# One gate transfer per group of eight experts, and activations weighed two at a time in column blocks one to four

## The chip, the cores and the metric

The kernel runs on one core of one Trainium2 chip. The metric is the device time of one execution in microseconds (us); lower is better. The kernel as it stands takes 3545.93 us (median of three runs). A profile of one further execution is used for all readings of the trace.

## The reference

A decoder block on 1024 tokens with 1024 channels: two token mixers (chunked retention and a short gated convolution), then a product-key expert retrieval layer (PEER), a per-layer embedding gate and a final norm. Only the PEER layer matters here. For each token eight heads choose 16 experts each out of 16384 and give them softmax gates; then

```python
def block(args):
    xb, ib, gb = args                    # tokens, chosen experts, their gates
    ue = jnp.take(u, ib, axis=0)
    act = jax.nn.gelu(jnp.einsum('td,ted->te', xb, ue), approximate=False)
    ve = jnp.take(v, ib, axis=0)
    return jnp.einsum('te,ted->td', (gb * act), ve)
```

## The kernel before, in words

The 1024 tokens are split. For 384 of them the rows of u and v that they chose are gathered one by one and multiplied on VectorE ("dots"). For the other 640 the layer is computed densely: the 16384 experts are 128 tiles of 128. A tile here is what the text calls an expert. A first stage multiplies every u tile with the 640 tokens, takes the GELU and writes the result (128 x 640, 320 KB) to `act_d` in DRAM. The gates of those tokens, zero for experts that were not chosen, are in `gate_d` in DRAM, laid out as block of 32 tokens, partition, expert, token.

The second stage is the one around the change. It takes the experts in 16 groups of eight (`NGRP`, `EG`), and for each group makes eight column blocks of the output (`dt` 0 to 7; one column block is called a step). In a step TensorE does 48 matmuls (line L1037: eight experts, high and low halves of a float32, two halves of the tokens) into one of two PSUM buffers `main`, and VectorE adds it into the result (`drain`, L2190). While the steps of group b run, the activations of group b+1 are made ready, expert by expert, through one PSUM buffer (`h_ps`, shown as `scr` in the trace):

1. SyncE loads the activation from `act_d` (`load_act`, L608), and ScalarE copies it to PSUM (`h_stage`, L1438).
2. VectorE multiplies it with the gates in `gate_in` (`weigh`, L2179).
3. ScalarE rounds it to the high half (`h_cast`, L1442).
4. VectorE subtracts for the low half (`lo_of_group`, L2184). Only then may `h_stage` of the next expert begin.

Which experts are treated in which step is a table:

```python
WEIGH_AT = ((), (0,), (1,), (2, 3), (4,), (5,), (6, 7), ())
```

The engines work through lists written out by hand, in order. VectorE, per step: drain, then for each expert in the table weigh, one dot (L1807), low half; then the remaining dots of the step (264 dots over 123 steps). ScalarE, per step: `h_stage` of the first expert in the table, then in even steps `v_cast` (L1429) of the two v tiles that TensorE needs two steps later, then `h_cast` of that expert, then the second expert if there is one. GpSimd waits for those casts, makes the low halves of the two v tiles (`v_lo`, L733) and then issues the gathers of rows for the next dots (L686). SyncE loads the next v tile (L568, 512 KB) when a low half is made, and between those loads the activations. Three times (before steps 8 and 72 and at 125) TensorE also turns back a block of the gathered tokens (L1015), which VectorE adds (L2197).

The gates of a group come on ScalarE's queue in two transfers of 1280 KB, each into its own half of the buffer: `load_gates(b + 1, 0)` behind `h_cast` of expert 3, `load_gates(b + 1, 1)` behind `h_cast` of expert 7 (L1421). Before the second stage, the gates of group 0 are read in five parts (L1483).

Of the kernel before, what the change touches and what calls it, by code (L numbers as in the profile page):

```python
# [23 lines left out]
F32 = mybir.dt.float32  # L24
# [3 lines left out]
ALU = mybir.AluOpType  # L28
# [3 lines left out]
P = 128  # L32
# [12 lines left out]
NE = NKEYS  # L45
# [25 lines left out]
TB = 32  # L71
NBLK = TDN // TB
EG = 8
HG = EG // 2
NGRP = NE // EG
# [20 lines left out]
GATE_PARTS = 5  # L96
# [1 line left out]
LAST_ROWS = 2 * S1 + NE - 3  # L98
SHIFT_ROWS = 2 * S1 + NE - 16
FIRST_H = NE - EG  # L100
WEIGH_AT = ((), (0,), (1,), (2, 3), (4,), (5,), (6, 7), ())
ROW_STEPS = V_STEPS - 5


# [55 lines left out]
def filled(step):  # L160

    return 8 + step + sum(1 for at in TURNS if at < step)
# [110 lines left out]
def build(nc, x_t, p_t, stream, u_rows, v_rows, key_t, gains, conv_c, rope, head_c, shape_c, out_t,  # L273
          score_d, act_d, gate_d, res_d):
    with ExitStack() as ctx:
        def sem(name):
            return ctx.enter_context(nc.semaphore(name))
# [26 lines left out]
        lay = region(const0)  # L304
# [10 lines left out]
        lay = region(ring0)  # L315
# [3 lines left out]
        lay = region(set1)  # L319
        a_hi, a_lo = [None] * 2, [None] * 2  # L320
        mix_hi, mix_lo = [None] * 2, [None] * 2
        for ps in range(2):
            lay = region(set1)
            a_hi[ps] = lay(f"a_hi{ps}", [P, DC, WIDTH[ps]], F32R)
            a_lo[ps] = lay(f"a_lo{ps}", [P, DC, WIDTH[ps]], F32R)
            lay = region(set2)
            mix_hi[ps] = lay(f"mix_hi{ps}", [P, DC, WIDTH[ps]], F32R)
            mix_lo[ps] = lay(f"mix_lo{ps}", [P, DC, WIDTH[ps]], F32R)
        lay = region(res0)
# [3 lines left out]
        for k, w in enumerate((TS, TDN, T)):  # L333
            lay = region(tmp0)
            nt0.append(lay(f"nt0_{k}", [P, w], F32))
            rowb.append(lay(f"rowb{k}", [P, 4, w], F32))
            if k < 2:
                lay = region(tmp0)
# [11 lines left out]
        for ps in range(2):  # L350
            w, n = WIDTH[ps], CHUNKS[ps]
            lay = region(set2)
# [10 lines left out]
            lay = region(set2 + 12 * w * 4)  # L363
            y.append(lay(f"y{ps}", [P, 2, w], F32))
            g.append(lay(f"g{ps}", [P, 2, w], F32))
        lay = region(set2 + 40 * 1024)
# [5 lines left out]
        lay = region(set2 + 48 * 1024)  # L372
        atok = [lay(f"atok{t}", [P, D], F32) for t in range(2)]
        s_ix = lay("s_ix", [P, NS, PH, 3 * TOPK], U32)
        lay = region(set2 + 61 * 1024)
        s_gate = lay("s_gate", [P, NS, P], F32)
        s_dot = lay("s_dot", [P, NS, P], F32)
        lay = region(set2 + 30 * 1024)
        keys0 = lay("keys0", [P, 2 * PH, NKEYS], F32)
        lay = region(tmp0 + 12800)  # L380
# [5 lines left out]
        lay = region(set1 + 40 * 1024)  # L386
        sc = lay("sc", [P, NS, 2 * PH, NKEYS], F32)
        lay = region(set1 + 40 * 1024)
# [5 lines left out]
        lay = region(set1)  # L394
        scores = lay("scores", [P, PH * 2, NKEYS], F32)
        gbuf = [lay(f"gbuf{i}", [P, NKEYS, TB], F32) for i in range(2)]
        lay = region(set1 + 2 * K4)
# [4 lines left out]
        lay = region(tmp0)  # L402
# [15 lines left out]
        for u in range(2):  # L418
            at = set1 if u == 0 else set2
            lay = region(at)  # L420
# [3 lines left out]
            lay = region(at + 40 * 1024)  # L424
# [1 line left out]
            v_lo.append(lay(f"v_lo{u}", [P, 2, D], F32R))  # L426
        v_raw = nc.alloc_sbuf_tensor_at("v_raw", [P, PRE, D], F32, offset=set1 + 48 * 1024)
        lay = region(tmp0)
        gate_in = [lay(f"gate_in{i}", [P, NBLK, HG, TB], F32) for i in range(2)]
        lay = region(set2 + 14 * K4)  # L430
        p_raw = lay("p_raw", [P, 2, T], F32)
        lay = region(set1 + 8 * K4)
        ple = lay("ple", [P, DC, T], F32)
        fg = nc.alloc_sbuf_tensor_at("fg", [P, 2, T], F32, offset=set1)
        lay = region(set1)
# [4 lines left out]
        lay = region(set2)  # L440
# [105 lines left out]
        v_hi_made = sem("v_hi_made")  # L546
        v_split = sem("v_split")
        act_in = [sem(f"act_in{k}") for k in range(EG)]
        gate_ins = [sem("gate_ins0"), sem("gate_ins1")]
        h_staged = sem("h_staged")  # L550
        h32_ready = sem("h32_ready")
        hhi_ready = sem("hhi_ready")
        h_ready = sem("h_ready")
        b_filled = sem("b_filled")
# [10 lines left out]
        @block.sync  # L565
        def _(sp):
            def load(pair, s):
                sp.dma_start(raw[:, s, :], stream[bass.ds(2 * pair + s, 1)].rearrange("a p n -> p (a n)")) \  # L568
                    .then_inc(raw_in[s], 16)

            def load_x(ps):
                for c in range(DC):
                    sp.dma_start(res[:, c, START[ps]:START[ps] + WIDTH[ps]],
                                 x_t[c * P:(c + 1) * P, START[ps]:START[ps] + WIDTH[ps]]).then_inc(x_in[ps][c], 16)

            def load_rope(ps):
                for dst, row in ((cos, 0), (sin, 1)):
                    sp.dma_start(dst[ps][:, :], rope[row, :, START[ps]:START[ps] + WIDTH[ps]]).then_inc(rope_in[ps], 16)

            load_x(0)  # L580
            load(0, 0)
            sp.dma_start(gain[:, :, :], gains).then_inc(consts_in, 16)
            load(0, 1)
            sp.dma_start(ident[:, :], shape_c[0]).then_inc(consts_in, 16)
            sp.dma_start(iota[:, :], shape_c[1]).then_inc(consts_in, 16)
            sp.dma_start(convc[:, :, :], conv_c).then_inc(consts_in, 16)
            load_rope(0)
            load_x(1)
            load_rope(1)
            with sp.Fori(1, S1) as pair:  # L590
                for s in range(2):
                    sp.wait_ge(tile_split, 2 * pair + s - 1)
                    load(pair, s)
            with sp.Fori(0, S1) as i:
                for s in range(2):
                    sp.wait_ge(tile_split, 2 * S1 + 2 * i + s - 1)
                    load(i, s)
            with sp.Fori(S1, B_PAIR - S1) as row:
                for s in range(2):
                    sp.wait_ge(tile_split, 2 * S1 + 2 * row + s - 1)  # L600
                    load(row, s)


            for s in range(2):
                sp.wait_ge(tile_split, 2 * B_PAIR + s - 1)
                load(B_PAIR - S1 + PRE // 2, s)
            def load_act(b, k):
                sp.dma_start(h32[b % 2][:, k, :], act_d[EG * (b - 1) + k]).then_inc(act_in[k], 16)  # L608

            sp.wait_ge(tile_done, 2 * B_PAIR)  # L610
            for q in act_st:
                sp.wait_ge(q, 16 + 16 * (FIRST_H // 2))
            for n in range(PRE + 2, NE + 2):
                b, place = divmod(n - 4, EG)
                if 0 <= place < 6 and n >= 4 and b + 1 < NGRP:
                    if place == 0:
                        if b:
                            sp.wait_ge(b_filled, filled(EG * b))
                        load_act(b + 1, 0)
                        load_act(b + 1, 1)  # L620
                    else:
                        load_act(b + 1, place + 1)
                        if place == 5:
                            load_act(b + 1, place + 2)
                sp.wait_ge(v_split, n - 1)
                load(B_PAIR - S1 + n // 2, n % 2)
            for t in range(2 * DC):
                sp.wait_ge(tile_split, F_TILE + t - 1)
                load(F_PAIR - S1 + t % DC // 2, t % 2)
            for half in range(2):  # L630
                at = slice(half * HALF, (half + 1) * HALF)
                for c in range(DC):
                    sp.wait_ge(out_ready, DC * half + c + 1)
                    sp.dma_start(out_t[c * P:(c + 1) * P, at], res[:, c, at]).then_inc(out_st, 16)
            sp.wait_ge(out_st, 16 * 2 * DC)
# [469 lines left out]
        def _(act):  # L1105
# [310 lines left out]
                act.wait_ge(dot_done, P * (t + 1))  # L1416
                act.activation(s_dot[:, t, :], s_dot[:, t, :], ACT.Gelu).then_inc(s_gelu, 1)

            def load_gates(b, half):
                at = EG * (b - 1) + HG * half  # L1420
                act.dma_start(gate_in[half][:, :, :, :].rearrange("p b e t -> p b (e t)"),  # L1421
                              gate_d[:, :, at:at + HG, :].rearrange("b p e t -> p b (e t)")) \
                    .then_inc(gate_ins[half], 16)

            def v_cast(n):
                if n >= 4:
# [13 lines left out]
            def h_cast(b, k):  # L1440
                act.wait_ge(h32_ready, EG * b + k + 1)
                act.copy(h_hi[b % 2][:, k, :], h_ps[:, 0:TDN]).then_inc(hhi_ready, 1)  # L1442
                if k % HG == HG - 1 and b + 1 < NGRP:
                    load_gates(b + 1, k // HG)

            swap_at = min(m for m in range(16 * ND) if due(2 * S1 + tile_of(m) - 1) > 2 * P)
            for e in range(NE):
# [5 lines left out]
                if e > FIRST_H:  # L1453
                    h_cast(0, e - FIRST_H - 1)
                if e >= FIRST_H:
                    h_stage(0, e - FIRST_H)
                j, k = divmod(e - LEAD, SPAN)
# [21 lines left out]
                first = e - (LEAD + SPAN * (ND - 1) + QUARTERS[15] + 2)  # L1479
                for part in range(2 * first, min(2 * first + 2, GATE_PARTS)) if first >= 0 else ():  # L1480
                    blocks = slice(NBLK * part // GATE_PARTS, NBLK * (part + 1) // GATE_PARTS)
                    for half in range(2):
                        act.dma_start(gate_in[half][:, blocks, :, :].rearrange("p b e t -> p b (e t)"),  # L1483
                                      gate_d[blocks, :, FIRST_H + HG * half:FIRST_H + HG * (half + 1), :].rearrange("b p e t -> p b (e t)")) \
                            .then_inc(gate_ins[half], 16)
                if e == NE - 8:
                    act.wait_ge(dot_done, LAST_LOW + 1)
                    for k in range(PRE):
# [1 line left out]
                if NE - PRE - 3 <= e < NE - 3:  # L1490
                    k = e - (NE - PRE - 3)
# [13 lines left out]
            for b in range(NGRP):  # L1505
                for dt in range(DC):
                    step = DC * b + dt
                    if step - 1 in ENDS:
                        sums_out(ENDS.index(step - 1))
                    ks = WEIGH_AT[dt] if b + 1 < NGRP else ()  # L1510
                    for k in ks[:1]:
# [60 lines left out]
            for t in range(2 * DC):  # L1572
                half, n = divmod(t, DC)
                at, s = slice(half * HALF, (half + 1) * HALF), t % 2
# [15 lines left out]
        def _(dve):  # L1590
# [580 lines left out]
                        hots(16 * (j + 1), w)  # L2171

            def weigh(b, k):
                half = k // HG
                if k % HG == 0:
                    dve.wait_ge(gate_ins[half], 16 * (b + GATE_PARTS))
                dve.wait_ge(h_staged, EG * b + k + 1)
                h3 = h_ps[:, 0:TDN].rearrange("p (b t) -> p b t", t=TB)
                dve.tensor_tensor(h3, h3, gate_in[half][:, :, k % HG, :], ALU.mult).then_inc(h32_ready, 1)  # L2179

            def lo_of_group(b, k):
                u = b % 2
# [26 lines left out]
            for step in range(V_STEPS - DC):  # L2209
                b, dt = divmod(step, DC)  # L2210
# [70 lines left out]
            for t in range(2 * DC):  # L2281
                half, n = divmod(t, DC)
                at, s = slice(half * HALF, (half + 1) * HALF), t % 2
# [108 lines left out]
```

## Time and profile before

| | |
|---|---|
| median of 3 runs | 3545.93 us (3545.28 to 3547.40) |
| profiled execution, its own time | 3540.74 us |
| span in the profile | 3538.9 us |
| TensorE busy | 3391.1 us, 96% |
| VectorE, ScalarE, GpSimd busy | 2532.9, 1287.8, 2175.7 us |
| granted TensorE clock, mean | 0.983 of full speed |
| second stage of the PEER layer (L1037) | from 2467.5 to 3381.9 us |

The profiled execution spent 1.8 us outside its span. In the timeline rows the columns are start, duration, engine, line, operation, written tile from read tile, and in brackets the idle time before it with what ended it. DMA packets are counted per queue: q0 holds the gathered rows, q1 what SyncE issues, q10 what ScalarE issues.

### The profile page before, as it was taken

Reading aid. Unit: us, or ns where it says so; the run is one execution under the profiler, and the core shown is the slowest. Engines: PE = TensorE matmul, PEld = TensorE weight load, DVE = VectorE, ACT = ScalarE, POOL = GpSimd, SP = SyncE. Lnnn points to the kernel's source line nnn. Section 1 sums busy time; section 2 is a strip of 40 time slices with the busy share of each in tenths; the row PEclk is TensorE's granted clock in tenths of the full one; section 3 lists DMA queues with packets and bytes.
Section 4 is the critical chain, followed back from the end, with each engine's and each line's share of the span. In section 5 each row is a group of like instructions: output and inputs, shape, how many; then the busy total and the mean of one; then the engine's idle time right before and its main releaser. Section 6 shows DMA issues by size and latency. Waiting matters only on the chain.

```text
span 3538.9 us, 58475 instructions
## 1 busy us (share of the span) xinstructions
PE 3391.1 (96%) x22379; PEld 3332.5 (94%) x22379; DVE 2532.9 (72%) x4232; ACT 1287.8 (36%) x2013; POOL 2175.7 (61%) x1426
## 2 busy tenths in 40 slices
PE   7899989998999989999999999999999999999987
PEld 6899979988999979999999999999999999999975
DVE  5615467668887667898989899754667676767567
ACT  3310131232121232456565655653333333333242
POOL 5578865332678656566666666765566665666544
PEclk9999989999999999999999999999999999999998
DMA  4233432111589868789898988988999998999712
GB/s 153 81 116 122 136 114 79 57 50 60 184 311 316 279 218 310 252 306 335 306 331 309 328 313 311 319 299 284 337 318 334 341 321 304 320 333 320 271 48 95
DMA packets 324309, 851.18 MB, mean 241 GB/s; under 512 B 27665, under 2 KB 125457, under 8 KB 320785
## 3 DMA queue, kind: packets, MB, share of 16 engines
q0 software_dynamic: 110592, 402.70, 31.2%
q1 hardware_dynamic: 92160, 300.62, 25.6%
q10 hardware_dynamic: 121360, 145.25, 12.2%
q8 instruction: 122, 2.00, 0.2%
q14 instruction: 75, 0.61, 0.0%
HBM read 756.20 MB, written 92.27 MB: 240 GB/s over the span
## 4 chain that ended last, share of the span: by engine, by line
PE 84%; DVE 10%; ACT 2%; issue 2%; DMA 1%; POOL 1%; ACTq 0%; DVEq 0%; SPq 0%; POOLq 0%
PE main L777 53%; PE main L1037 24%; PE scr L975 4%; DMA rows<-v_rows,s_idx 1%; DVE rows L1800 1%; PE scr L875 1%; PE scr L792 1%; DVE rowb L1624 1%; PE main L1079 1%; PE scr L816 0%; DVE res L2286 0%; DVE y L1884 0%; PE scr L820 0%; DVE rowb L2010 0%; DVE rowb L1600 0%
## 5 line engine op out<-in xcount | busy, mean ns | idle before, releaser
L653 POOL TENSOR_TENSOR w_lo<-raw,w_hi 128x1024 fp32r<-128x1024 f32 x206 | 534.3, 2594 | 421.9 <-ACT w_hi L1132 417.9
L777 PE MATMUL main<-mix_hi,w_hi 128*128 128x320 f32 (+1 forms) x2816 | 685.2, 317 | 29.8 <-DVE mix_lo L1632 9.9
L777 PE MATMUL main<-mix_lo,w_hi 128*128 128x320 f32 (+1 forms) x2816 | 673.2, 313 | 0.0
L777 PE MATMUL main<-mix_hi,w_lo 128*128 128x320 f32 (+1 forms) x2816 | 673.1, 313 | 0.0
L1807 DVE SCALAR_TENSOR_TENSOR scr<-rows,s_dot,scr 128x1024 f32<-128x1024 f32 x381 | 489.0, 1284 | 167.0 <-DMA rows<-v_rows,s_idx 150.6
L777 PEld LDWEIGHTS main<-mix_hi,w_hi 128*128 128x128 f32 x2816 | 476.8, 190 | 34.5 <-issue 19.6
L777 PE MATMUL main<-a_hi,w_hi 128*128 128x320 f32 (+1 forms) x1728 | 465.8, 324 | 24.2 <-DVE a_lo L1632 8.6
L686 POOL DMA_INDIRECT rows<-u_rows,s_idx x384 | 397.4, 1035 | 135.8 <-issue 69.0
L777 PEld LDWEIGHTS main<-mix_lo,w_hi 128*128 128x128 f32 x2816 | 480.3, 189 | 0.0
L777 PEld LDWEIGHTS main<-mix_hi,w_lo 128*128 128x128 f32 x2816 | 479.5, 189 | 0.0
L1037 PE MATMUL main<-h_hi,v_hi 128*128 128x320 f32 x2048 | 467.7, 310 | 9.3 <-issue 3.5
L1800 DVE CUSTOM_DVE_ANT_0 rows<-rows,scr 128x1024 f32<-128x1024 f32 x384 | 446.1, 1215 | 41.4 <-PE main L777 22.7
L1037 PE MATMUL main<-h_lo,v_hi 128*128 128x320 f32 x2048 | 467.4, 309 | 0.0
L1037 PE MATMUL main<-h_hi,v_lo 128*128 128x320 f32 x2048 | 467.0, 309 | 0.0
L733 POOL TENSOR_TENSOR v_lo<-raw,v_hi 128x1024 fp32r<-128x1024 f32 x126 | 301.8, 2415 | 264.3 <-ACT v_hi L1429 257.9
L777 PE MATMUL main<-a_lo,w_hi 128*128 128x320 f32 (+1 forms) x1728 | 458.9, 320 | 0.0
L777 PE MATMUL main<-a_hi,w_lo 128*128 128x320 f32 (+1 forms) x1728 | 458.3, 320 | 0.0
L686 POOL DMA_INDIRECT rows<-v_rows,s_idx x384 | 368.9, 961 | 126.8 <-issue 82.9
L1037 PEld LDWEIGHTS main<-h_hi,v_hi 128*128 128x128 f32 x2048 | 342.5, 188 | 10.5 <-issue 4.0
L1037 PEld LDWEIGHTS main<-h_hi,v_lo 128*128 128x128 f32 x2048 | 343.0, 188 | 0.0
L1037 PEld LDWEIGHTS main<-h_lo,v_hi 128*128 128x128 f32 x2048 | 343.0, 188 | 0.0
L777 PEld LDWEIGHTS main<-a_hi,w_hi 128*128 128x128 f32 x1728 | 302.9, 190 | 32.6 <-issue 19.0
(270 smaller groups left out, 5137.4 us busy)
## 6 DMA issues: line engine op xcount, KB each, us to landing
raw<-stream SPq DMA_DIRECT2D x480, 512.0 KB
gate_d<-gbuf ACTq DMA_DIRECT2D x20, 2048.0 KB, 8.9
act_d<-actb ACTq DMA_DIRECT2D x120, 320.0 KB
gate_in<-gate_d ACTq DMA_DIRECT2D x30, 1280.0 KB
h<-act_d SPq DMA_DIRECT2D x120, 320.0 KB
rows<-u_rows,s_idx POOLq DMA_INDIRECT x384
rows<-v_rows,s_idx POOLq DMA_INDIRECT x384
score_d<-stage ACTq DMA_DIRECT2D x16, 320.0 KB
```

What stands on the lines that cost most here:

```text
L653: pool.tensor_tensor(w_lo[:, s, :], raw[:, s, :], w_hi[:, s, :].bitcast(F32), ALU.subtract) \
L686: pool.indirect_dma_start(rows[HOMES[k]][:, :], None, table[:, :], bass.IndirectOffsetOnAxis(ap=s_idx[:, t, n:n + 1], axis=0)) \
L733: pool.tensor_tensor(v_tile(v_lo, n), raw[:, n % 2, :], v_tile(v_hi, n).bitcast(F32), ALU.subtract).then_inc(v_split, 1)
L777: last = pe.matmul(main[s][:, dst:dst + n], wt[:, s, c * P:(c + 1) * P], rows[:, c, src:src + n], start=(c == 0 and wt is w_hi and rows is ...
L792: last = pe.matmul(slot[:, at:at + n], ones[:, :], src[:, at:at + n], start=True, stop=True)
L875: last = pe.matmul(slot[:, t * P:(t + 1) * P], qrow[ps][:, s, t * P:(t + 1) * P], row_of(keys[ps], 2 * h + s), start=True, stop=True)
L975: last = pe.matmul(scr[1][:, w * HALF + k * P:w * HALF + (k + 1) * P], hot_key(half + w, 1, k), hot_key(half + w, 0, k), start=True, stop= ...
L1037: last = pe.matmul(slot[:, half * HALF:half * HALF + HD], v_tile(vt, n)[:, col:col + P], ht[u][:, k, half * HD:(half + 1) * HD], start=(k ...
L1079: last = pe.matmul(main[s][:, half * HALF:(half + 1) * HALF], wt[:, n // 4, col:col + P], pt[:, c, half * HALF:(half + 1) * HALF], start=( ...
L1624: dve.scalar_tensor_tensor(rowb[ps][:, c % 4, :], res_row(c, ps), gain[:, which, c:c + 1], nt0[ps][:, :], ALU.mult, ALU.mult).then_inc(row ...
L1800: dve.tensor_tensor_reduce(got[:, :], got[:, :], acc[:, :], 1.0, 0.0, ALU.mult, ALU.add, s_dot[:, t, n:n + 1]).then_inc(dot_done, 1)
L1807: dve.scalar_tensor_tensor(acc[:, :], got[:, :], s_dot[:, t, n:n + 1], acc[:, :], ALU.mult, ALU.add).then_inc(dot_done, 1)
```

## The change

One buffer holds the gates of all eight experts of a group, and one transfer of 2560 KB fills it, issued behind `h_cast` of expert 7. In `gate_d` the eight experts of a token block lie together on a partition, so a run in DRAM is 1024 bytes where it was 512; their number per transfer, 20 blocks x 128 partitions, stays 2560. VectorE waits for the gates once per group, before expert 0. Experts are treated in pairs in steps 1, 2, 3 and 4, none in steps 5, 6, 7 and 0. SyncE issues the activation loads in pairs, between the v tiles n = 8b+4 to 8b+7. The five parts for group 0 are one transfer each.

```diff
-WEIGH_AT = ((), (0,), (1,), (2, 3), (4,), (5,), (6, 7), ())
+WEIGH_AT = ((), (0, 1), (2, 3), (4, 5), (6, 7), (), (), ())
...
-        gate_in = [lay(f"gate_in{i}", [P, NBLK, HG, TB], F32) for i in range(2)]
+        gate_in = lay("gate_in", [P, NBLK, EG, TB], F32)
...
-                if 0 <= place < 6 and n >= 4 and b + 1 < NGRP:
-                    if place == 0:
-                        if b:
-                            sp.wait_ge(b_filled, filled(EG * b))
-                        load_act(b + 1, 0)
-                        load_act(b + 1, 1)
-                    else:
-                        load_act(b + 1, place + 1)
-                        if place == 5:
-                            load_act(b + 1, place + 2)
+                if place < HG and b + 1 < NGRP:
+                    if b and place == 0:
+                        sp.wait_ge(b_filled, filled(EG * b))
+                    for k in range(2 * place, 2 * place + 2):
+                        load_act(b + 1, k)
...
-            def load_gates(b, half):
-                at = EG * (b - 1) + HG * half
-                act.dma_start(gate_in[half][:, :, :, :].rearrange("p b e t -> p b (e t)"),
-                              gate_d[:, :, at:at + HG, :].rearrange("b p e t -> p b (e t)")) \
-                    .then_inc(gate_ins[half], 16)
+            def load_gates(b):
+                at = EG * (b - 1)
+                act.dma_start(gate_in[:, :, :, :].rearrange("p b e t -> p b (e t)"),
+                              gate_d[:, :, at:at + EG, :].rearrange("b p e t -> p b (e t)")).then_inc(gate_ins, 16)
...
-                if k % HG == HG - 1 and b + 1 < NGRP:
-                    load_gates(b + 1, k // HG)
+                if k == EG - 1 and b + 1 < NGRP:
+                    load_gates(b + 1)
...
-                    for half in range(2):
-                        act.dma_start(gate_in[half][:, blocks, :, :].rearrange("p b e t -> p b (e t)"),
-                                      gate_d[blocks, :, FIRST_H + HG * half:FIRST_H + HG * (half + 1), :].rearrange("b p e t -> p b (e t)")) \
-                            .then_inc(gate_ins[half], 16)
+                    act.dma_start(gate_in[:, blocks, :, :].rearrange("p b e t -> p b (e t)"),
+                                  gate_d[blocks, :, FIRST_H:NE, :].rearrange("b p e t -> p b (e t)")) \
+                        .then_inc(gate_ins, 16)
...
             def weigh(b, k):
-                half = k // HG
-                if k % HG == 0:
-                    dve.wait_ge(gate_ins[half], 16 * (b + GATE_PARTS))
+                if k == 0:
+                    dve.wait_ge(gate_ins, 16 * (b + GATE_PARTS))
                 dve.wait_ge(h_staged, EG * b + k + 1)
                 h3 = h_ps[:, 0:TDN].rearrange("p (b t) -> p b t", t=TB)
-                dve.tensor_tensor(h3, h3, gate_in[half][:, :, k % HG, :], ALU.mult).then_inc(h32_ready, 1)
+                dve.tensor_tensor(h3, h3, gate_in[:, :, k, :], ALU.mult).then_inc(h32_ready, 1)
```

## Rows read from the trace of the kernel before

**Rows 1.** The page: span and TensorE's busy time.

```profile
span 3538.9 us, 58475 instructions
...
PE 3391.1 (96%) x22379; PEld 3332.5 (94%) x22379; DVE 2532.9 (72%) x4232; ACT 1287.8 (36%) x2013; POOL 2175.7 (61%) x1426
```

**Rows 2.** Busy time from 3100 to 3156 us, eight steps (then clock, DMA share, GB/s).

```profile
3100.00:3156.00 56.00, 56.00 (x384) 56.00 (x383) 39.34 (x42) 18.70 (x24) 34.91 (x25) 1.00 0.95 326
```

**Rows 3.** All waits of TensorE between 2467 and 3368 us.

```profile
PE main L1037 <- issue: 3.5, 2, 2.7
PE main L1037 <- DVE res L2197: 3.4, 1, 3.4
PE main L1037 <- DVE res L2190: 2.4, 1, 2.4
```

**Rows 4.** Timeline of VectorE, steps 3, 4 and 5 of group 1.

```profile
2556.08 0.82 DVE L2190 TENSOR_TENSOR res<-main,res 128x640 f32<-128x640 f32 x1 [2.36 <-issue]
...
2560.38 0.83 DVE L2179 TENSOR_TENSOR scr<-scr,gate_in 128x640 f32<-128x640 f32 x1 [0.82 <-ACT scr L1438]
...
2563.12 0.82 DVE L2190 TENSOR_TENSOR res<-main,res 128x640 f32<-128x640 f32 x1
...
2570.16 0.82 DVE L2190 TENSOR_TENSOR res<-main,res 128x640 f32<-128x640 f32 x1 [1.68 <-PE main L1037]
```

**Rows 5.** Timeline of ScalarE, steps 3 and 6 of group 1 and after.

```profile
2561.26 0.37 ACTq L1421 DMA_DIRECT2D gate_in<-gate_d  x1
2563.22 0.70 ACT L1438 COPY scr<-h 128x640 f32<-128x640 f32 x1 [1.27 <-DVE h_lo L2184]
2563.85 1.99 ACT L1429 CAST v_hi<-raw 128x1024 fp32r<-128x1024 f32 x2
...
2583.38 0.37 ACTq L1421 DMA_DIRECT2D gate_in<-gate_d  x1
```

**Rows 6.** Timeline of GpSimd, behind those two casts.

```profile
2564.97 4.79 POOL L733 TENSOR_TENSOR v_lo<-raw,v_hi 128x1024 fp32r<-128x1024 f32 x2 [8.03 <-ACT v_hi L1429]
```

**Rows 7.** Timeline of VectorE, group 2: step 1 (expert 0 weighed) and step 4.

```profile
2598.32 0.82 DVE L2190 TENSOR_TENSOR res<-main,res 128x640 f32<-128x640 f32 x1 [3.63 <-PE main L1037]
2599.07 0.82 DVE L2179 TENSOR_TENSOR scr<-scr,gate_in 128x640 f32<-128x640 f32 x1
...
2620.34 0.83 DVE L2179 TENSOR_TENSOR scr<-scr,gate_in 128x640 f32<-128x640 f32 x1
```

**Rows 8.** DMA queues from 2562 to 2568.5 us: packets, MB, share of the engines.

```profile
q10 hardware_dynamic: 2576, 1.31, 74.2%
```

**Rows 9.** DMA queues from 2568.5 to 2585 us.

```profile
q0 software_dynamic: 767, 2.81, 48.3%
q1 hardware_dynamic: 856, 2.72, 45.0%
```

**Rows 10.** DMA queues from 2585 to 2589 us.

```profile
q10 hardware_dynamic: 463, 0.24, 22.1%
```

**Rows 11.** DMA queues from 2589 to 2603 us.

```profile
q0 software_dynamic: 753, 2.76, 49.4%
q1 hardware_dynamic: 834, 2.29, 42.1%
q10 hardware_dynamic: 965, 0.49, 12.1%
```

**Rows 12.** DMA queues from 2603 to 2607.5 us.

```profile
q10 hardware_dynamic: 1148, 0.58, 47.2%
```

**Rows 13.** Timelines of ScalarE and VectorE at the first group's end and step 1 of group 0.

```profile
2470.55 0.38 ACTq L1421 DMA_DIRECT2D gate_in<-gate_d  x1
...
2483.40 0.82 DVE L2179 TENSOR_TENSOR scr<-scr,gate_in 128x640 f32<-128x640 f32 x1
...
2490.45 1.29 DVE L1807 SCALAR_TENSOR_TENSOR scr<-rows,s_dot,scr 128x1024 f32<-128x1024 f32 x1 [4.31 <-DMA rows<-v_rows,s_idx]
```

**Rows 14.** VectorE's waits for gathered rows between 2467.5 and 3368 us.

```profile
DVE scr L1807 <- DMA rows<-v_rows,s_idx: 93.5, 48, 7.1
```

More of the change, by code:

```diff
@@ L548, in build @@
         act_in = [sem(f"act_in{k}") for k in range(EG)]
-        gate_ins = [sem("gate_ins0"), sem("gate_ins1")]
+        gate_ins = sem("gate_ins")
         h_staged = sem("h_staged")
```

## The prediction

> **What bounds the kernel now.** I read four views. The page first: TensorE is busy for 96% of the span [rows 1]. Then busy time by stretch, to see whether that holds where the change is: over eight steps of the second stage TensorE is busy for all 56.00 us, VectorE for 39.34 of them, ScalarE for 18.70, while the DMA engines are busy for 95% of the time [rows 2]. So TensorE sets the pace, and the transfers are the resource nearest to becoming the limit. Third, TensorE's waits from 2467 to 3368 us: 3.5 + 3.4 + 2.4 = 9.3 us [rows 3]. A rearrangement can win back no more than that in this stage, 0.26% of the run. The question is therefore what it can lose. Fourth, timelines and DMA counts of groups 1 and 2, for the cover behind each wait. Within 0.2%, about 7 us, counts as no change from here on: that is about what a measurement of this kernel can tell.
>
> **What the work of a step costs.** One step of TensorE is 7.04 us (VectorE's drain at 2598.32 waited for TensorE, and drains follow at that pace: 2563.12 to 2570.16) [rows 4, 7]. A step in which two experts are weighed costs VectorE the same: drain at 2556.08, first next drain at 2563.12, so 7.04 us, two dots included [rows 4]. Four pairs in a row thus leave VectorE no slack in steps 1 to 4, where steps 1, 2, 4 and 5 had one expert before; steps 5, 6, 7 and 0 become light. The number of weighings, copies, casts and dots is unchanged, so busy time changes by nothing. A step with a third dot (18 of 123, as there are 264 dots) takes one dot more, about 1.3 us by the duration of a dot [rows 13].
>
> What hangs on VectorE's time in a pair: ScalarE's `h_stage` for the next step waits for the second low half, and `v_cast` is queued behind it. After the pair of step 3 the copy is at 2563.22 and the casts at 2563.85 [rows 5], GpSimd makes the two low halves in 4.79 us from 2564.97 [rows 6], the first being ready near 2567.4, and TensorE wants it near 2570.0, when the step ends whose drain is at 2570.16 [rows 4]. The margin is 2.6 us (the second tile, wanted half a step later, has 3.7). Before, the casts after a pair came at one tight place in this form; now they come at two, in steps 2 and 4. With gates in time a margin of 2.6 us covers one late third dot. Drains have more room: one is needed a step after it can start, 7.0 - 0.8 = 6.2 us.
>
> **The transfer, the part that decides.** Before: the transfer behind expert 3 left at 2561.26 and had landed by 2568.5; its 2560 packets of 512 bytes met empty queues (with their 16 small ones they are 74.2% of the engines' time in 6.5 us) [rows 5, 8]. Its first user is at 2599.07 [rows 7]: 30.6 us of cover. The transfer behind expert 7 left at 2583.38, right before the next group's activations, v tiles and rows, and its last 1148 packets passed from 2603 to 2607.5 [rows 5, 12]; 24 us. Its user is at 2620.34 [rows 7]: 13 us of cover.
>
> After: one transfer, behind expert 7, now the second of step 4. The same place in step 3 is 2561.26; one step later is 2568.3. Its first user is expert 0 of the next group at 2599.07. So it has 30.8 us. How far does it get? The packets are again 2560 (plus 16), of 1024 bytes. A packet of 512 costs 6.5 x 16 x 0.742 / 2576 = 30 ns of an engine; a kilobyte is bounded by 30 (size is free) and 60 ns (all is size). Gathered rows of 4 KB cost 16.5 x 16 x 0.483 / 767 = 166 ns, 41 per KB, so 50 is nearest; that is 20 ns x 160 = 3.2 us more per engine than one old transfer, and 1.6 us less than two.
>
> What it meets, in packets on q10:
>
> - 2568.5 to 2585, 16.5 us: the other queues pass 767 and 856 packets there with no gates present, at 93% [rows 9]. Two of the activation loads move out of it. Where all queues have work the counts of the three are alike: 753, 834 and 965 in 14 us [rows 11]. So the gates get about one packet for each of q0's, 767; or, if the free 7% (1.1 us, at 50 ns 350 packets) is theirs too, 1110.
> - 2585 to 2589: 463 were passed [rows 10]; with the larger size I take 430.
> - 2589 to 2599.07: 965 in 14 us is 69 per us [rows 11], so 10.07 us give 694, or 650 for the larger size.
>
> Sum: 767 + 430 + 650 = 1850 to 1110 + 463 + 694 = 2267 of 2576. What is missing, 309 to 726, goes at 69 per us: the gates are late by 4.5 to 10.5 us. A second bound: the engines had worked off everything by 2607 [rows 12]; 3.2 us more work, less 1.1 us of idle time used, puts that at 2609, 10 us after the need. I take 7 us.
>
> The Trainium skill, page "DMA: Bandwidth & Descriptors", section "Queues, rings and completion order", says that each engine goes round the queues packet by packet, and that such a packet is typically 9 to 17 descriptors. Here the counts show one for one at the granularity of the trace; if the gates' turn were a bundle of 9 and a row's turn one descriptor, they would land within a few us of the issue and the sum below would be zero. Rows 11 speak against that.
>
> **What late gates cost.** VectorE stops at `weigh` of expert 0 in step 1. Behind it stand the dot, expert 1, the next drain. ScalarE stops at `h_cast` of expert 0, and behind it stand expert 1 and the casts of step 2; behind these GpSimd's low halves and gathers. Since step 1 is now a pair, those casts have the margin of 2.6 us. TensorE therefore waits 7 - 2.6 = 4.4 us at step 4 (bounds: 4.5 - 2.6 = 1.9 and 10 - 2.6 = 7.4). VectorE stays 2.6 us behind through the pairs and recovers in step 5, so each group repeats it. Groups 2 to 15 have such a transfer: 14 x 4.4 = 62 us (27 to 104).
>
> Group 1 is by itself: its whole transfer leaves where the second half did, at 2470.55, and is wanted at 2483.40 [rows 13], 12.9 us later, with the reload of `res` behind it on the same queue. Some 160 packets per engine x 20 ns make it about 4 us late; part of that is covered, as VectorE waited 4.31 us for a row soon after [rows 13]. Bounds 0 and 4; I take 3.
>
> Gained: with light steps 5 to 7 VectorE should be nearer to time at the turns, where the waits of rows 3 lie; 0 to 9.3, and I take 3, because those waits hang on gathered rows (93.5 us of waits for them [rows 14]), which the gates now delay. The other edits cost nothing: activations are loaded earlier or at the same time, used earlier by at most two steps, and expert 1 is now wanted a step sooner but loaded with expert 0; the parts for group 0 leave with five issues less on ScalarE's queue while TensorE works through the first stage; if they were late, it would cost a few us once, and I leave that to the range.
>
> Sum against the profiled execution's 3540.7 (span 3538.9 and 1.8 around it): 3540.7 + 62 + 3 - 3 = 3603. The median of the runs is 5.2 us above that execution, so 3608.
>
> **Rivals.**
> (a) The gates are in time, or late by less than 2.6 us. For it: they start 15 us before the old second transfer did, and could take all idle DMA time; they need 83 packets per us and the mix gave 69, quiet stretches 400. Then TensorE sees nothing: 3546, within 7.
> (b) Faster, on the other side: gates in time and VectorE on time at both turns, so that the 9.3 us of rows 3 go: 3546 - 9 = 3537. It decides only if the gates take less than 30.8 + 2.6 = 33.4 us in every group and the rows at steps 6 and 7 are not later than before.
> (c) Gates in time, but the unbroken pairs carry VectorE's delay (third dots, late rows) past 2.6 us at the casts of steps 2 and 4: about 1 us in 14 groups, 3560. Against it: rows are waited for in light steps mostly.
> (d) The delay feeds on itself: 2.6 us behind at step 4, the next transfer starts 2.6 us later and lands at the bound of 10 us: 14 x 7.4 = 104, 3650.
>
> **How the numbers follow.** Forecast (late gates, 27 to 85 us, own range 3570 to 3632) 0.50; (d) 0.10; (c) 0.13; (a) 0.19; (b) 0.08. Slower 0.50 + 0.10 + 0.13 = 0.73, same 0.19, faster 0.08. The range leaves out (b) and half of (d) with the edges: 3541 to 3645.
>
> **What would show it.** Right: TensorE waits once in each group before its fifth step, released by GpSimd's low half of v; VectorE idle before the weighing in step 1, released by the gates' transfer, 7 us more than before; gates landing some 37 us after issue; groups of 60 to 61 us where there were 56.3. Wrong: gates landing in under 33 us, that is q10 passing over 83 packets per us beside full queues; or casts that are not behind the pair in time.

## The result, and the profile after

The changed kernel takes 3678.20 us (median of 4 runs, 3665.03 to 3685.74), the kernel before, on the same chip, 3546.66 us (3545.28 to 3548.85): 131.5 us more, a ratio of 1.0371, interval 1.0355 to 1.0387. The forecast was 3608 with a range to 3645. The sign was right; the size was twice the forecast and outside the range. The profiled execution took 3665.03 us, 124.3 more than the one before. Four slow executions far above the others of their kernel (one in experiment 9, two in experiment 11, one of the kernel before beside them) are left out of medians and ratios.

First the page of the changed kernel, to be held against [rows 1], with the group of TensorE's matmuls of the second stage and the DMA issues (size, median us to landing).

```profile
span 3663.0 us, 58439 instructions
...
PE 3419.2 (93%) x22379; PEld 3355.0 (92%) x22379; DVE 2538.3 (69%) x4232; ACT 1288.1 (35%) x2013; POOL 2170.2 (59%) x1426
...
L1032 PE MATMUL main<-h_hi,v_hi 128*128 128x320 f32 x2048 | 481.7, 317 | 99.5 <-POOL v_lo L728 87.5
...
gate_in<-gate_d ACTq DMA_DIRECT2D x15, 2560.0 KB, 38.4
```

The waits of TensorE, VectorE, ScalarE and GpSimd from 2467 to 3500 us (us in total, times, longest), against [rows 3] and [rows 14].

```profile
PE main L1032 <- POOL v_lo L728: 87.5, 21, 10.1
PE main L1032 <- DVE res L2182: 11.0, 3, 6.1
...
DVE scr L1800 <- DMA rows<-v_rows,s_idx: 199.3, 101, 7.4
DVE scr L2171 <- DMA gate_in<-gate_d: 99.0, 14, 11.0
...
ACT h_hi L1436 <- DVE scr L2171: 287.9, 91, 18.9
ACT v_hi L1423 <- DMA raw<-stream: 230.1, 59, 9.7
...
POOL v_lo L728 <- ACT v_hi L1423: 378.2, 61, 20.7
```

What the reader is to see: VectorE waits for gates once in each of 14 groups, 7.1 us in the mean; the gates land 38.4 us after their issue. TensorE waits for low halves of v, where before it waited 9.3 us for everything. But the waits for gathered rows have more than doubled too, 199.3 us for 93.5, and ScalarE waits 230.1 us for v tiles to land. More than the gates is late.

One such place in the changed kernel, VectorE and ScalarE around the step where expert 0 is weighed, against [rows 7].

```profile
3333.99 0.82 DVE L2182 TENSOR_TENSOR res<-main,res 128x640 f32<-128x640 f32 x1
3344.29 0.83 DVE L2171 TENSOR_TENSOR scr<-scr,gate_in 128x640 f32<-128x640 f32 x1 [9.47 <-DMA gate_in<-gate_d]
```

```profile
3305.14 0.37 ACTq L1416 DMA_DIRECT2D gate_in<-gate_d  x1
...
3345.15 0.69 ACT L1436 CAST h_hi<-scr 128x640 fp32r<-128x640 f32 x1 [16.99 <-DVE scr L2171]
...
3351.32 1.99 ACT L1423 CAST v_hi<-raw 128x1024 fp32r<-128x1024 f32 x2
```

The chain is the one foretold: gates, weighing, ScalarE's cast of `h`, its cast of v. Then busy time of that place by stretch (length, then TensorE, its weight loads, VectorE, ScalarE, GpSimd, and at the end clock, DMA share, GB/s).

```profile
3337.00:3345.00 8.00, 8.00 (x57) 8.00 (x56) 0.71 (x1) 0.00 (x0) 0.00 (x0) 1.00 0.84 330
3347.00:3355.00 8.00, 0.21 (x2) 0.10 (x1) 6.36 (x8) 4.75 (x7) 2.56 (x2) 0.74 0.00 0
3355.00:3361.00 6.00, 6.00 (x23) 6.00 (x24) 5.34 (x6) 2.62 (x4) 4.95 (x4) 0.50 0.85 300
3361.00:3364.00 3.00, 3.00 (x22) 3.00 (x22) 2.18 (x4) 1.13 (x2) 0.93 (x1) 0.99 0.98 344
```

TensorE stands for 8 us, and for the 6 us after that its granted clock is 0.50, 1.2 GHz: 23 matmuls where 43 would fit at the full clock of 2.4 GHz, so about 2.8 us are lost a second time. The DMA engines move nothing in the 8 us, because every queue that could feed them is behind ScalarE.

The 124.3 us are lost in the stage. These are its stretches, in the kernel before and in the changed one:

```profile
2467.50:3382.60 915.10, 906.55 (x6168) 905.30 (x6168) 622.48 (x645) 302.75 (x380) 566.55 (x398) 1.00 0.90 314
```

```profile
2470.00:3508.70 1038.70, 939.49 (x6168) 932.71 (x6168) 627.37 (x645) 303.25 (x380) 564.88 (x398) 0.95 0.76 278
```

The stage is 123.6 us longer. TensorE's waits in it are 99.8 us (the 99.3 above, 0.5 before a transpose) less 9.3, so 90.5 more; its busy time is 939.5 for 906.6 with the same 6168 matmuls, so 32.9 more, at a mean clock of 0.95 for 1.00. Ahead of the stage the changed kernel is 2.5 us later, behind it 2.0 us shorter. (On the whole page the busy time differs by 28.1 us only, as outside the stage it is 4.8 us less.)

### The profile page after: what moved, and what is told of

Same layout as the page of the kernel before. It is cut to its first block, busy times and chain, and to the rows that moved or that the text cites. A ratio compares the mean times of both kernels' runs of the same rounds, so it can differ in the third digit from the quotient of the medians.

```text
span 3663.0 us, 58439 instructions
## 1 busy us (share of the span) xinstructions
PE 3419.2 (93%) x22379; PEld 3355.0 (92%) x22379; DVE 2538.3 (69%) x4232; ACT 1288.1 (35%) x2013; POOL 2170.2 (59%) x1426
## 4 chain that ended last, share of the span: by engine, by line
PE 57%; DVE 16%; DMA 16%; ACT 5%; issue 3%; POOL 2%; ACTq 0%; DVEq 0%; SPq 0%; POOLq 0%
PE main L772 48%; DMA gate_in<-gate_d 14%; PE scr L970 4%; DVE scr L1800 3%; DMA rows<-v_rows,s_idx 2%; PE main L1032 2%; DVE h_lo L2176 2%; POOL v_lo L728 1%; ACT v_hi L1423 1%; ACT scr L1432 1%; DVE rows L1793 1%; PE scr L870 1%; DVE res L2278 1%; PE scr L787 1%; DVE rowb L1617 1%
## 5 line engine op out<-in xcount | busy, mean ns | idle before, releaser
L1032 PE MATMUL main<-h_hi,v_hi 128*128 128x320 f32 x2048 | 481.7, 317 | 99.5 <-POOL v_lo L728 87.5
L1032 PE MATMUL main<-h_lo,v_hi 128*128 128x320 f32 x2048 | 478.1, 315 | 0.0
L1032 PE MATMUL main<-h_hi,v_lo 128*128 128x320 f32 x2048 | 476.3, 314 | 0.0
L1032 PEld LDWEIGHTS main<-h_hi,v_hi 128*128 128x128 f32 x2048 | 352.2, 194 | 106.0 <-issue 94.0
L1032 PEld LDWEIGHTS main<-h_lo,v_hi 128*128 128x128 f32 x2048 | 353.5, 194 | 0.0
L1032 PEld LDWEIGHTS main<-h_hi,v_lo 128*128 128x128 f32 x2048 | 352.2, 193 | 0.0
## 6 DMA issues: line engine op xcount, KB each, us to landing
gate_in<-gate_d ACTq DMA_DIRECT2D x15, 2560.0 KB, 38.4
```

The costliest lines, as they stand in the source:

```text
L1032: last = pe.matmul(slot[:, half * HALF:half * HALF + HD], v_tile(vt, n)[:, col:col + P], ht[u][:, k, half * HD:(half + 1) * HD], start=(k ...
```

## The experiments

Each was run beside the kernel before on the same chip; the medians of the latter were 3540.2, 3542.2, 3537.2 and 3543.5 us in the four sessions. "Casts" are those of v tiles.

**1. Undo the single transfer.** The gates again in two halves and two buffers (behind experts 3 and 7); table and activation loads as changed.

```diff
-                if k == EG - 1 and b + 1 < NGRP:
-                    load_gates(b + 1)
+                if k % HG == HG - 1 and b + 1 < NGRP:
+                    load_gates(b + 1, k // HG)
```

> The changed kernel with the gates in two transfers and two buffers again, as before (behind experts 3 and 7, now in steps 2 and 4). Pairs in steps 1 to 4 and the paired activation loads stay. Theory T (the single transfer lands after its first user, and everything follows from that): the first half leaves some 45 us ahead of its user and the second, wanted by expert 4 in step 3, some 45 us too; TensorE's waits on v_lo (87.5 us in the changed kernel) go to under 10, the time is 3546 within 10 us. Rival P (the unbroken pairs leave VectorE no slack, so the casts behind them are late whatever the gates do): most of the loss stays, 3600 or more.

Measured: 3620.02 us, ratio 1.0229 (1.0203 to 1.0255). My theory missed: some 50 us come back, 80 stay, though no wait for gates is left. TensorE's waits in it:

```profile
PE main L1032 <- POOL v_lo L728: 47.9, 15, 6.4
PE main L1032 <- DVE res L2185: 10.5, 4, 5.2
```

and the place where it starts, VectorE in the pair of step 3 (the first line is the weighing of expert 5):

```profile
3191.69 0.83 DVE L2174 TENSOR_TENSOR scr<-scr,gate_in 128x640 f32<-128x640 f32 x1 [0.82 <-ACT scr L1433]
3196.85 1.29 DVE L1802 SCALAR_TENSOR_TENSOR scr<-rows,s_dot,scr 128x1024 f32<-128x1024 f32 x1 [4.32 <-DMA rows<-v_rows,s_idx]
3198.04 0.82 DVE L2179 TENSOR_TENSOR h_lo<-scr,h_hi 128x640 fp32r<-128x640 f32 x1
```

A dot between `weigh` and the low half waits 4.32 us for its row; the casts of step 4 stand behind that low half.

**2. The single transfer alone.** The kernel before with one buffer and one transfer behind expert 7, in step 6.

```diff
-                if k % HG == HG - 1 and b + 1 < NGRP:
-                    load_gates(b + 1, k // HG)
+                if k == EG - 1 and b + 1 < NGRP:
+                    load_gates(b + 1)
```

> The kernel before with only the transfer changed: one buffer, one transfer of 2560 KB behind expert 7, which there is in step 6. Old table of experts, old activation loads. The transfer then has some 16 us to its first user, where the changed kernel gives it 31. Theory T: VectorE waits for gates in each of 14 groups, by 12 to 20 us; the casts of step 2 have a margin of 6 us there (one expert in step 1), so TensorE waits 6 to 12 us per group and its clock falls after each: 3660 to 3760. Rival P: without the unbroken pairs nothing is lost, 3546 within 10.

Measured: 3664.89 us, 1.0353 (1.0331 to 1.0376), as my theory has it; VectorE waits 160.6 us for gates in 15 groups, 10.7 each. So either half of the change costs by itself: the transfer without the table 3.5%, the table without the transfer 2.3%, both 3.7%. They don't add, which suggests that they share a path. But this is not quite the changed kernel's transfer: it leaves two steps later, 13 to 22 us ahead of its user in place of some 30.

**3. No gates.** The changed kernel, transfers of gates left out from group 1 on (all groups take those of group 0).

> The changed kernel without any gate transfer in the second stage: all groups are weighed with the gates of group 0 (so part of the computation is left out). Pairs and loads stay. Theory T: no waits on v_lo, and 8 us less DMA work per group: 3530 to 3548. Rival P: 3600 or more, as the pairs are all there.

Measured: 3533.23 us, 0.9982 (0.9965 to 0.9998). The pairs, with the casts behind them, cost nothing when neither the traffic of the gates nor a wait for them is there. Rival P as I had put it, no slack by VectorE's own pace, falls.

**4. Same bytes, same time, twice the packets.**

```diff
-                at = EG * (b - 1)
-                act.dma_start(gate_in[:, :, :, :].rearrange("p b e t -> p b (e t)"),
-                              gate_d[:, :, at:at + EG, :].rearrange("b p e t -> p b (e t)")).then_inc(gate_ins, 16)
+                for half in range(2):
+                    at = EG * (b - 1) + HG * half
+                    act.dma_start(gate_in[:, :, HG * half:HG * (half + 1), :].rearrange("p b e t -> p b (e t)"),
+                                  gate_d[:, :, at:at + HG, :].rearrange("b p e t -> p b (e t)")).then_inc(gate_ins, 16)
```

> The changed kernel with its one transfer made as two of 1280 KB, both issued in the place of the one and both waited for before expert 0: the same bytes at the same time, as 5120 packets of 512 bytes. If a queue gets turns by packet beside the others (my reading of rows 11), the gates land later still, up to the point where all queues are empty: VectorE's wait for gates grows from 7.1 us a group to 9 to 13, the time to 3700 to 3740. Rival B (queues share by bytes, or the DMA engines' total is all that counts): only the packets' own price, 1.7 us a group or less, 3678 to 3700.

Measured: 3711.19 us, 1.0496 (1.0459 to 1.0534), 33 us above the changed kernel (39.5 if each is held against the kernel before that ran beside it), in the span foretold; VectorE waits 133.1 us for gates, 10.2 in each of 13 groups. Rival B's bound, 1.7 us a group or 24 in all, is passed, but not by much, with one profile of each kernel: this speaks for turns by packet and does not prove them. The changed kernel's own counts speak for them too, where all three queues had work (3322 to 3332 us):

```profile
q0 software_dynamic: 565, 2.06, 52.1%
q1 hardware_dynamic: 487, 1.33, 34.6%
q10 hardware_dynamic: 562, 0.57, 17.0%
```

**5. Casts ahead.** In the changed kernel the casts of steps 2 and 4 move on ScalarE's list to steps 1 and 3, behind the first `h_stage` and ahead of the first `h_cast`. Nothing else.

```diff
-                    if dt % 2 == 0:
-                        for n in range(step + 2, min(step + 4, NE)):
-                            v_cast(n)
+                    ahead = b + 1 < NGRP and dt in (1, 2, 3, 4)
+                    for n in (3, 4) if ahead and dt % 2 else (2, 3) if not ahead and dt % 2 == 0 else ():
+                        if step + n < NE:
+                            v_cast(step + n)
```

> The changed kernel with the casts of v tiles moved on ScalarE's list: those of steps 2 and 4 stand in steps 1 and 3, behind the first h_stage and ahead of the first h_cast, so that no pair stands ahead of them. The gate transfer stays single and late. If the loss goes by way of the casts queued behind the pair, TensorE's waits on v_lo (87.5 us) fall under 15; what stays are late drains, 10 us of lateness less 6.2 of room, and a dot or cast more in a pair: 3580 to 3620. If the late gates hold TensorE by another way (drains alone), the waits only change their name: 3660 or more.

Measured: 3553.37 us, 1.0029 (1.0015 to 1.0044). Of 131 us some 120 are back, with the single transfer in place. More than I expected, and for another reason: I had taken the gates' lateness as given and looked only at who waits behind them. VectorE's waits in this kernel:

```profile
DVE scr L1801 <- DMA rows<-v_rows,s_idx: 17.4, 11, 4.5
DVE scr L2172 <- DMA gate_in<-gate_d: 9.8, 2, 7.2
```

The gates are late in two groups only, and rows are waited for a tenth of the time. GpSimd's timeline shows what moved. In the changed kernel, over one group:

```profile
3286.29 4.68 POOL L728 TENSOR_TENSOR v_lo<-raw,v_hi 128x1024 fp32r<-128x1024 f32 x2 [20.74 <-ACT v_hi L1423]
...
3301.14 4.78 POOL L728 TENSOR_TENSOR v_lo<-raw,v_hi 128x1024 fp32r<-128x1024 f32 x2 [5.34 <-ACT v_hi L1423]
...
3310.75 2.42 POOL L728 TENSOR_TENSOR v_lo<-raw,v_hi 128x1024 fp32r<-128x1024 f32 x1
...
3322.78 2.42 POOL L728 TENSOR_TENSOR v_lo<-raw,v_hi 128x1024 fp32r<-128x1024 f32 x1
```

and with the casts ahead:

```profile
3159.30 4.78 POOL L728 TENSOR_TENSOR v_lo<-raw,v_hi 128x1024 fp32r<-128x1024 f32 x2 [2.36 <-ACT v_hi L1423]
...
3173.18 2.42 POOL L728 TENSOR_TENSOR v_lo<-raw,v_hi 128x1024 fp32r<-128x1024 f32 x1 [4.27 <-ACT v_hi L1423]
...
3190.32 4.79 POOL L728 TENSOR_TENSOR v_lo<-raw,v_hi 128x1024 fp32r<-128x1024 f32 x2 [4.93 <-ACT v_hi L1423]
...
3203.17 4.79 POOL L728 TENSOR_TENSOR v_lo<-raw,v_hi 128x1024 fp32r<-128x1024 f32 x2 [2.92 <-ACT v_hi L1423]
```

Behind each pair of low halves stand four or five gathers of 512 KB and, through SyncE, two v loads. In the changed kernel GpSimd stands for 20.74 us; the low halves of step 4 follow at 3301.14, their gathers leave from 3306.05 to 3309.80, and the gates leave in the same moment, at 3305.14. With the casts ahead the same low halves are at 3190.32, their gathers leave from 3195.25 to 3199.31, and only then the gates, at 3201.46. So the gates find the queues nearly empty for a while. The DMA queues between 3 and 9 us after an issue of the gates, with the casts ahead (issue at 3144.4) and in the changed kernel (issue at 3305.1):

```profile
q10 hardware_dynamic: 1835, 1.88, 95.4%
q1 hardware_dynamic: 58, 0.24, 10.3%
q0 software_dynamic: 22, 0.05, 2.2%
```

```profile
q10 hardware_dynamic: 785, 0.80, 46.7%
q0 software_dynamic: 166, 0.64, 26.5%
q1 hardware_dynamic: 144, 0.52, 22.7%
```

It is so in every group. In the first 10 us after the issue, q10 passes 1605 to 2133 packets with the casts ahead and 1091 to 1220 in the changed kernel (14 transfers each, all but the first group's); the last packet passes 17.5 to 27.2 us after the issue, once 31.9, in place of 27.2 to 41.2. Whether it is the gathers or the v loads that have to be out of the way, no run separates.

**6. The activation loads alone.** The kernel before with SyncE's new order of loads.

> The kernel before with only SyncE's new order of activation loads (pairs, earlier); old table, old gate transfers. If the earlier loads crowd the queues where rows and gates pass, VectorE's waits for rows rise from 93 us and the time by 10 us or more. My theory: they are hidden, 3540 within 5.

Measured: 3545.09 us, 1.0008 (0.9993 to 1.0024); waits for rows 96.2 us, as before. This part of the change is free.

**7. Halves and casts ahead.** The edit of 5 on the kernel of 1.

> The kernel of the first run (two halves, pairs) with the casts of steps 2 and 4 moved ahead of the pairs as well. In the first run TensorE still waited 47.9 us for v_lo, since a dot inside a pair waited for its row and the casts stood behind it. Theory C (the casts and the gathers queued behind them are the way of the loss, and the pairs alone have no price): back to 3540 within 10. Rival P (the pairs have a price by VectorE's own pace): 3580 or more.

Measured: 3537.14 us, 0.9992 (0.9976 to 1.0008). Theory C holds; the pairs have no price.

**8. The first half leaves one step later.** The kernel of 1 with

```diff
-                if k % HG == HG - 1 and b + 1 < NGRP:
-                    load_gates(b + 1, k // HG)
+                if k in (5, 7) and b + 1 < NGRP:
+                    load_gates(b + 1, k // 7)
```

> The kernel of the first run with the first half of the gates issued behind expert 5 (step 3) in place of expert 3 (step 2), the second behind expert 7 as there. In the first run the first half left together with the burst of row gathers behind the casts of step 2 and the rows of step 4 came late. If that meeting on the queues is what costs, the rows of step 4 are in time, VectorE's delay at steps 4 to 6 falls from 6 us to under 3, and the time from 3620 to under 3575. If only the order of the casts matters, it stays above 3600.

Measured: 3558.16 us, 1.0048 (1.0029 to 1.0067), from 3620. The casts stand where they stood and no transfer is smaller; only the half of the gates no longer leaves with the burst of gathers behind the casts of step 2. TensorE's waits for low halves fall from 47.9 to 6.9 us. The total of VectorE's waits for rows falls only from 211.1 to 166.8 us, as most of it lies in steps that weigh nothing; but the part behind expert 5's weighing, where the row above lies, falls from 54.2 to 0.7. So for these rows it is the meeting on the queues that makes them late, and the order of casts that carries the delay on.

**9 and 10. Which casts.** The changed kernel with only the casts of step 2 ahead, and with only those of step 4.

```diff
+                    casts = range(2, 4) if dt % 2 == 0 else ()
+                    if b + 1 < NGRP and dt in (1,):     # the other kernel: (3,)
+                        casts = range(3, 5)
+                    if b + 1 < NGRP and dt in (2,):     # the other kernel: (4,)
+                        casts = ()
```

> The changed kernel with only the casts of step 2 moved ahead of the first h_cast of step 1; those of step 4 stay behind the pair of step 3. Theory F (a cast behind a late pair makes its v tiles and the gathers behind them late, that bunches the transfers, and the bunch makes the next gates late): one place of two is left, and VectorE, once late, is still late at step 3, so the wait moves from step 4 to step 6 and is smaller: 3580 to 3640. Rival M (only the casts right behind the gate wait matter, the ones of step 2): all is won back, 3555 or less.

> The changed kernel with only the casts of step 4 moved ahead of the first h_cast of step 3; those of step 2 stay behind the pair of step 1, and with it behind the gate wait. Theory F: the wait at step 4 stays, a little smaller as the transfers are bunched less: 3600 to 3670. Rival M: nothing changes, 3670 to 3685.

Measured: step 2 only 3683.98 us, 1.0413 (1.0372 to 1.0453); step 4 only 3558.29 us, 1.0069 (1.0045 to 1.0092). Both outside what I wrote, and rival M fails as clearly. With only step 2 ahead TensorE's waits change their name, from low halves to drains, as the casts are served but VectorE still stands at the gates for 119.1 us (in most groups TensorE's wait at step 4 is the weighing's lateness less 6.2 us, the room that the prediction gave the drains):

```profile
PE main L1032 <- DVE res L2187: 84.3, 19, 8.4
PE main L1032 <- POOL v_lo L728: 24.9, 14, 3.4
```

With only step 4 ahead the wait for gates is 27.4 us in 9 groups and TensorE's for low halves 13.3. The casts of step 4 are those whose transfers start last ahead of the gates. Behind the pair they start with the gates and make them late; ahead of it they are on their way when the gates leave. Theory F's loop, in which one group's late gates are what makes the next group's late, is not needed for this, and both its numbers missed. In the changed kernel, too, the one group that did not wait for its gates (expert 0 weighed at 3003.79) was followed by a transfer that took 38.9 us (issued at 3037.1).

**11. The same edit on the kernel before.** Casts of step 4 ahead of their pair.

> The kernel before with the casts of step 4 moved ahead of its pair in step 3, the one place where it has casts behind a pair at the narrow margin. All else as before. Theory F: rows are waited for less (93 us before), and as TensorE waits only 9 us in this stage the time gains at most that: 3532 to 3542. Rival N (the order is of no use where nothing is late): within 2 us of before.

No verdict: only two runs count, 3537.13 and 3546.89 us, and the runs before beside them took 3535.11 to 3548.55. Waits for rows fell from 93.5 to 48.2 us, as foretold; what that is worth is open, and under 0.3%.

**12. Kernel 7 once more, five rounds.**

> The kernel with two halves, pairs and the casts of steps 2 and 4 ahead, once more with more rounds, as the best of all versions: its one profile shows 3.9 us of TensorE's waits in the second stage where the kernel before has 9.3. If those 5 us are all there is, the ratio to before is 0.9985 within 0.001; if they were chance, it is 1.000.

Measured: 3538.72 us for 3543.51, 0.9987 (0.9978 to 0.9996), and TensorE's waits in the stage are 3.8 us. It is ahead of the kernel before by 0.13% here; in experiment 7 the interval of the same kernel took in 1.

## Why the prediction was right and wrong

**What bounds the kernel.** Right: at most 9.3 us could be won [rows 3]; the best version won 4.8.

**Cost of the parts.** The activation loads cost nothing (6), the pairs by themselves cost nothing (3, 7). The margins are seen at work, 2.6 us for casts behind a pair in the changed kernel and 6.2 for drains in experiment 9. Rival (c), late rows inside a pair with the gates in time, did not come up in the changed kernel, whose gates were late. But experiment 1 shows its mechanism, and at 80 us where (c) had 14: with the gates in time the casts behind the pair are still late.

**The transfer.** The forecast was 37.8 us from issue to landing and 7 us of waiting; measured 38.4 and 7.1. Rivals (a) and (b) fell with it. The way of counting turns fits what experiment 4 and the counts above show. That it gave the right landing was in part luck: experiments 5 and 10 have the same transfer at the same place among the same bytes, and VectorE waits 9.8 and 27.4 us for gates in all, where it waited 99.0. Which transfers have just started when it leaves decides, and the prediction took that from counts of the kernel before and never asked it of the new order.

**The step that failed: "TensorE therefore waits 7 - 2.6 = 4.4 us at step 4", 62 us in 14 groups, as the whole price.** The mechanism is right: in 13 of the 14 groups the trace has TensorE's wait at step 4 at the weighing's lateness less 2.6 to 2.7 us (10.4 late, 7.8 waited, at the place shown above; 12.7 and 10.1 in the worst group; 2.5 and nothing in another). Lateness is counted here from 7.8 us after the end of TensorE's step 0, where an undelayed weighing of expert 0 starts, as the one at 2599.07 in [rows 7]. The sum is wrong in three terms:

- The clock, put at nothing without a word. The same matmuls took 32.9 us more. This was the largest miss, over a quarter of the loss. In the profiled execution the waits alone, 90.5 us, would have stayed inside the range (bound: 104).
- The wait at step 4: 78.2 us for 62, that is 5.6 in each of 14 groups. The weighing is 7.8 us late in the mean, 0.9 of it because VectorE is already late when it arrives (up to 2.5), and unevenly so, from 0 to 12.7; a group that is early gives nothing back.
- Everything else that TensorE waits for in the stage: 21.6 us, where it was 9.3 and the forecast had +3 and -3. Of it 11.0 are late drains, the longest (6.1) before step 8.

Together 78.2 + 21.6 - 9.3 + 32.9 = 123.4, and the stage is 123.6 us longer. Rival (d), at 0.10, came nearest in number (7.4 us a wait, 3650), but its reason, a delay that feeds on itself, is not shown: the order of casts and gates suffices (experiments 9 and 10).

**What was left out altogether** was that my 2.6 us of margin, which I had found, could be changed by a line's order. With the casts ahead the pairs cost nothing (7) and the single transfer, pairs and all, costs 0.3% (5).

**Group 1 and the turns.** I had +3 and -3. In the changed kernel TensorE waited 4.4 us for low halves in group 0, so the +3 (bounds 0 and 4) was near; in experiment 5 it waited 8.3 us there, for a drain. The turns were not relieved, as the drain before step 8 shows.

What stays open: why the gates land sooner in some groups of the changed kernel (27 to 34 us in three near the middle), which therefore lose little; why rows are waited for so much longer in steps that weigh nothing; and the 16 us that experiment 8 still loses.

## What to carry to other kernels

Where transfers take nearly all of the engines' time (90% in this stage), ask which other transfers start in the same moment as the one you move: how much traffic there is on the whole did not decide here, its order did. In an engine's list, look for instructions that feed transfers and stand behind others that may wait for one; here moving two casts in each of two steps was worth 120 us, and the transfer that looked like the cause, once they were moved, cost some 16 (3553 against 3537). And give every wait of TensorE its price in clock: here 90.5 us of waits came with 32.9 us of slower matmuls.

## What was not expected of the hardware

After three waits of TensorE of some 8 us its clock was granted at 0.50 for the next 6 us, as in the stretch from 3355 to 3361 us above; after the seven others of 5 us and more the mean of the next 6 us was 0.52 to 0.76. After the wait of one other group of the changed kernel, 2.15 us within 2895 to 2901, the next stretch shows 28 matmuls in 4 us at 1.00:

```profile
2895.00:2901.00 6.00, 3.85 (x27) 3.61 (x26) 5.18 (x6) 3.78 (x6) 2.55 (x2) 1.00 0.03 11
2901.00:2905.00 4.00, 4.00 (x28) 4.00 (x29) 3.42 (x4) 1.83 (x3) 3.56 (x3) 1.00 0.74 244
```

At these two places the short wait cost its length and the long one about 2.8 us more.

And 2560 KB took 38.4 us in the changed kernel, 68 GB/s, beside two other queues; over the whole of one such transfer the counts per queue were

```profile
q0 software_dynamic: 1859, 6.78, 43.6%
q1 hardware_dynamic: 1695, 5.02, 33.3%
q10 hardware_dynamic: 2576, 2.62, 22.1%
```

The queue with the smallest packets has the most of them and the least of the time.
